# Order of the opening stages, bank-wise evacuation and earlier weight splits in a one-core HGRN2 layer

## Chip, cores and metric
One NeuronCore of a Trainium2 chip runs the whole layer. The metric is the device time of one execution, in microseconds, as the median of the runs.

## What is computed
One layer of a bidirectional generator trunk, all in float32, for 256 latent tokens `x` and 256 context tokens `ctx` of width 2048:
```
shift, scale, gate, shift2, scale2, gate2 = split(silu(c) @ w_ada + b_ada, 6)   # context: silu(c_ctx)
a     = rms_norm(t, norm_mix) * (1 + scale) + shift          # for x and ctx
q,v,g = split(a @ w_in, 3);   z[d] = a @ w_f[d]              # d = forward, backward
log_f = log_sigmoid(clip(z)) + log1p(lb * exp(-z));  k = (1 - lb) * sigmoid(-z);  q = silu(q) / sqrt(128)
o     = scan of S_t = diag(f_t) S_{t-1} + k_t v_t^T, o_t = S_t^T q_t, both directions, 16 heads of 128
h     = x + gate * ((rms_norm(o, o_norm) * silu(g)) @ w_o)
h     = h + gate2 * swiglu(rms_norm(h, norm_ffn) * (1 + scale2) + shift2);  out = rms_norm(h, final_norm)
```
The context is scanned first and gives the latent scan its start states. The inner width of the SwiGLU is 5632.

## The kernel before
**Products in three parts.** Each weight block is read as float32 into one of four slots of `raw` (128 x 1024, 512 KB) and split into `whi` (ACT, `hi`, L426) and `wlo = raw - whi` (DVE, `lo`, L689), three slots each. Activations stand as `ahi` and `alo` (features x 512 tokens, 16 column groups k of 128). A product is hi*hi + hi*lo + lo*hi, three matmuls (`three`, L1121).

**Head.** The first four of the six parts of `w_ada` (64 blocks, `rb` 0 to 63) are streamed; 40 are split, and 24 (`ada_direct`, k mod 8 in 1, 4, 6) go whole from slots of their own to a plain float32 matmul (L1066). `mod_sum` (L1054) sums rows of the modulation for c and c_ctx. A quarter q is 16 blocks; the column is (q + 2) mod 4, so scale comes before shift. After a quarter, ACT copies the rows (`mod_rows`, L440), PE turns them (`turn_rows`, L1080), DVE adds the bias (`modulation`, L716). At rb 6 (`X_AT`) ctx and x tiles are loaded, squared on ACT (`x_rstd`), transposed on PE (`turn_x`) and copied to `xT` by DVE (L737). At rb 16 SP stores the transposed x to DRAM (L365, 2 MB; it is read back for the residual), and DVE multiplies `xT` by the row norm in place (L746), after that store. At rb 32 `keep` and `masks` are loaded. Before all that, PE waits for the identity, the bias rows, o_norm and six vector rows, and transposes them (L1094, L1095); DVE copies them out (L696, L697), and ACT makes silu(c) (L432). `modulate(k)` (L463) applies scale and shift (L469) and makes `ahi` (L472), `a_lo(k)` (L728) makes `alo`: k 0 to 7 beside rb 56 to 63, k 8 to 15 after the last quarter.

**Pairs.** Sixteen heads make eight pairs (`positions`, L93). A pair has 8 chunks "VQ" (two k each; values into banks 0 and 1, queries into bank 2) and 8 chunks "Z" (gates of two directions and two heads, banks 0 to 3, matmuls of 512 columns). C_B is the first chunk. Between VQ and Z, DVE copies the values out of banks 0 and 1 (`values`, L814, L819) and ACT the queries by SiLU with a table load before and after (`queries`, L521). After Z, DVE clips the four gate banks (`clip_gates`, L788, L793), ACT makes exponentials (`gate_exps`, `gate_sigmoid`), DVE log gates and keys (L796 to L812). The scan of a head is 13 steps j, one per chunk position (`scan` on each of three engines), two heads overlapping. Of these: DVE cumulates the gates and sums the keys (j=0, L885 to L896), builds level exponents (j=1, 2), multiplies levels (j=3, 4, L855) and operands (j=5, L907); PE turns keys and makes scores (j=6, 8, L1227, L1230), states (j=7), outputs (j=9, L1238); DVE places masked scores (`place`, L860, at j=7 and 9, seven copies L867) and scales outputs (j=12, L935). PE's part stands in the middle of a chunk.

**Order at a position.** The engines walk the same list. DVE: `lo(ck)`, gates and keys, scan steps, `ada(i)` (an accumulation for the other modulation rows, L783), then at the boundaries `values` or `clip_gates`. ACT: `hi(ck)`, gate exps, scan steps, then `queries`. `hi(ck)` waits until chunk ck-3 has been used. SP issues the loads in the order of `RING`: chunk ck, then the `ada` blocks of ck; a load waits until the block four places before has been consumed.

**Rest.** A gate stage "G" (32 chunks, from C_G), the output projection (from C_WO, `wide`), SwiGLU (from C_FF), its down projection, and the final norm. The tail of the heads' scans runs in G.

The code of the Z and VQ matmuls and the loop that calls them:

Of the kernel before, what the change touches and what calls it, by code (L numbers as in the profile page):

```python
# [19 lines left out]
F32 = mybir.dt.float32  # L20
# [36 lines left out]
DIRECT = 6  # L57
X_AT = 6
# [9 lines left out]
R_NMIX, R_NFFN, R_FIN, R_LB, R_C, R_CCTX, R_ONORM = 0, 16, 32, 48, 64, 80, 96  # L68
VROWS = 97
# [35 lines left out]
def build(nc, x, c, ctx, c_ctx, w_ada, b_ada, norm_mix, norm_ffn, lb_logits, w_in, w_f, o_norm, w_o,  # L105
# [12 lines left out]
    with stack:  # L118
# [14 lines left out]
        xin = arena[:, 0:4 * D].rearrange("p (t d) -> p t d", t=4)  # L133
        h1 = arena[:, 0:KF * T].rearrange("p (k t) -> p k t", k=KF)
# [37 lines left out]
        vrow = arena[:, 4 * D:4 * D + P]  # L172
        brow = arena[:, 4 * D + P:4 * D + 2 * P]
# [27 lines left out]
        s_vrow = sem("vector_rows_in")  # L201
        s_keep = sem("keep_and_masks_in")
# [25 lines left out]
        s_used = sem("chunk_used")  # L228

# [66 lines left out]
        def _(sp):  # L296
            sp.dma_start(ident[:, :], ident_in).then_inc(s_const, 16)
            sp.dma_start(brow[0:96, :], b_ada[0].rearrange("(k p) -> k p", p=P)).then_inc(s_const, 16)
            sp.dma_start(vrow[R_ONORM:R_ONORM + 1, :], o_norm).then_inc(s_const, 16)
# [18 lines left out]
            def load(ck):  # L318
# [3 lines left out]
                if ck < C_B:  # L322

                    q, k = divmod(SPLIT_ADA[ck], KD)
                    col = (q + 2) % 4 * CW
# [26 lines left out]
            def load_direct(j):  # L352
                if j >= DIRECT:
                    sp.wait_ge(s_du, j - DIRECT + 1)
                q, k = divmod(DIRECT_ADA[j], KD)
                col = (q + 2) % 4 * CW
# [17 lines left out]
            for ck in range(C_B, CHUNKS):  # L374
                load(ck)
                for i in ada_blocks(ck):
# [43 lines left out]
        def _(act):  # L420
# [7 lines left out]
            for r, v in ((R_C, c[0]), (R_CCTX, c_ctx), (R_NMIX, norm_mix[0]), (R_NFFN, norm_ffn[0]), (R_FIN, final_norm),  # L428
                         (R_LB, lb_logits[0])):
                act.dma_start(vrow[r:r + KD, :], v.rearrange("(k p) -> k p", p=P)).then_inc(s_vrow, 16)  # L430
            act.wait_ge(s_vec, 1)
            act.activation(cs[:, :, 0], vec[:, R_C:R_C + KD], ACT.Silu)  # L432
            act.activation(cs[:, :, 1], vec[:, R_CCTX:R_CCTX + KD], ACT.Silu).then_inc(s_cs, 1)
            act.wait_ge(s_cs, 1)
            act.activation(cs4[:, :, :, 0], cs[:, :, :], ACT.Copy).then_inc(s_c4, 1)
            act.preload_act_table_set(EXP_LN)
            act.wait_ge(s_lb, 1)
            act.activation(lbt[:, 1, :], lbt[:, 0, :], ACT.Exp).then_inc(s_lb, 1)
# [24 lines left out]
            def modulate(k):  # L463

                act.wait_ge(s_mod, 8 if k < 8 else 10)
                act.wait_ge(s_xn, k + 1)
                for i in range(2):
                    v = xT[:, k, i * T:(i + 1) * T]
# [3 lines left out]
                act.activation(ahi[:, k, :], xT[:, k, :], ACT.Copy).then_inc(s_ah, 1)  # L472

            for rb in range(4 * KD):
                if rb == X_AT:
                    x_rstd()
                if not ada_direct(rb % KD):
                    hi(SPLIT_ADA.index(rb))
                if rb == 10:
# [4 lines left out]
                if rb >= 4 * KD - 8:  # L484
                    modulate(rb - 4 * KD + 8)
# [7 lines left out]
            for i in range(6, KD // 2 + 1):  # L493
# [21 lines left out]
            def gate_sigmoid(pr, i):  # L515
# [3 lines left out]
                act.activation(K, K, ACT.Exp, scale=-1.0).then_inc(s_zk, 1)  # L519

# [86 lines left out]
            for k in range(KD):  # L607
# [6 lines left out]
                hi(C_WO + 2 * k)  # L614
                if k == 0:
# [70 lines left out]
        def _(dve):  # L686
# [8 lines left out]
            dve.wait_ge(s_vecT, 1)  # L695
            dve.tensor_copy(vec[:, :], mx[:, 0:VROWS]).then_inc(s_vec, 1)  # L696
            dve.tensor_copy(bias[:, :], mx[:, 128:224]).then_inc(s_vec, 1)  # L697

# [704 lines left out]
```

## Time and profile before
| | |
|---|---|
| median of 3 runs | 1943.01 us (1941.77 to 1945.99) |
| the profiled execution's own time | 1942.41 us |
| its span | 1940.1 us, mean granted clock 0.990 |
| instructions | 31876 |
| first matmul into a bank of a pair | 124.30 us |
| DMA | 353.18 MB, mean 182 GB/s |

The profile is of one execution. "Busy" is the union of an engine's instructions. Matmuls are pipelined, so a duration overlaps the next one; pace is the distance of starts. PEclk is the granted share of 2.4 GHz: 1.0 or, throttled, 0.5 (1.2 GHz). In lists of waits the engine after "<-" released the one before it. In timelines the bracket holds the idle time of the engine before the instruction and what ended it.

### The profile page before, as it was taken

How to read it: one execution, taken by the hardware profiler on the slowest of the kernel's cores; microseconds unless marked ns; L12 is line 12 of the kernel's file. 1: busy time of each engine (PE TensorE's matmuls, PEld its weight loads, DVE VectorE, ACT ScalarE, POOL GpSimd, SP SyncE). 2: the span in 40 equal slices, each digit the busy share in tenths (PEclk: the TensorE clock that was granted, in tenths of full speed). 3: DMA queues.
4: the chain of work that ended last, by engine and by line, in shares of the span. 5: the costliest groups of instructions: out<-in, count | busy, mean ns of one | idle time of the engine just before them, and what ended most of it. 6: DMA issues, size and time to landing. Idle time of an engine off the chain costs nothing.

```text
span 1940.1 us, 31876 instructions
## 1 busy us (share of the span) xinstructions
PE 1852.1 (95%) x13318; PEld 1689.8 (87%) x13318; DVE 1256.8 (65%) x1949; ACT 861.9 (44%) x1186; POOL 0.2 (0%) x4
## 2 busy tenths in 40 slices
PE   6989999999999999999889999999999999999998
PEld 2258989788989788888779989999999999999996
DVE  4754768686968787878985455555545555545445
ACT  4582535343545344545445454333333433444444
POOL 0000000000000000000000000000000000000000
PEclk9999999999999999999999999999999999999999
DMA  8965544443444444443655546777767676555552
GB/s 326 392 217 167 170 128 138 141 153 125 147 131 131 157 147 130 142 141 120 196 185 209 183 123 206 216 227 217 217 218 218 214 225 212 182 182 183 182 185 98
DMA packets 175377, 353.18 MB, mean 182 GB/s; under 512 B 12737, under 2 KB 80642, under 8 KB 174594
## 3 DMA queue, kind: packets, MB, share of 16 engines
q1 hardware_dynamic: 175042, 351.11, 56.2%
q8 instruction: 104, 1.70, 0.4%
q14 instruction: 39, 0.32, 0.1%
q10 hardware_dynamic: 192, 0.05, 0.0%
HBM read 346.92 MB, written 4.19 MB: 181 GB/s over the span
## 4 chain that ended last, share of the span: by engine, by line
PE 79%; DVE 14%; DMA 2%; issue 2%; ACT 2%; ACTq 0%; DVEq 0%
PE bank L1122 19%; PE bank L1123 19%; PE bank L1124 19%; DVE wlo L689 3%; DVE aacc L783 3%; PE score L1227 2%; PE bank L1159 2%; PE bank L1161 2%; PE bank L1160 2%; DMA raw<-in_w_ada_dram 2%; PE score L1122 1%; PE score L1123 1%; PE score L1124 1%; DVE work L867 1%; DVE work L837 1%
## 5 line engine op out<-in xcount | busy, mean ns | idle before, releaser
L1122 PE MATMUL bank<-ahi,whi 128*128 128x256 f32 (+1 forms) x2912 | 891.8, 306 | 34.7 <-DVE wlo L689 19.0
L1123 PE MATMUL bank<-alo,whi 128*128 128x256 f32 (+1 forms) x2912 | 882.7, 303 | 0.0
L1124 PE MATMUL bank<-ahi,wlo 128*128 128x256 f32 (+1 forms) x2912 | 882.4, 303 | 0.0
L689 DVE TENSOR_TENSOR wlo<-raw,whi 128x1024 fp32r<-128x1024 f32 x496 | 605.7, 1223 | 417.6 <-ACT whi L426 417.0
L426 ACT ACTIVATE whi<-raw 128x1024 fp32r<-128x1024 f32 x496 | 522.3, 1056 | 547.8 <-PE bank L1124 447.1
L1122 PEld LDWEIGHTS bank<-ahi,whi 128*128 128x128 f32 x2912 | 560.3, 192 | 63.8 <-DVE wlo L689 22.7
L1124 PEld LDWEIGHTS bank<-ahi,wlo 128*128 128x128 f32 x2912 | 560.3, 192 | 20.7
L1123 PEld LDWEIGHTS bank<-alo,whi 128*128 128x128 f32 x2912 | 560.6, 193 | 18.5
L1159 PE MATMUL bank<-whi,ahi 128*128 128x256 f32 x512 | 151.1, 295 | 16.0 <-DVE arena L793 9.9
L783 DVE SCALAR_TENSOR_TENSOR aacc<-raw,cs,aacc 128x1024 f32<-128x1024 f32 x120 | 153.5, 1279 | 0.5
L1161 PE MATMUL bank<-whi,alo 128*128 128x256 f32 x512 | 146.2, 285 | 0.0
L1160 PE MATMUL bank<-wlo,ahi 128*128 128x256 f32 x512 | 146.2, 285 | 0.0
L1159 PEld LDWEIGHTS bank<-whi,ahi 128*128 128x128 f32 x512 | 99.7, 195 | 20.9 <-issue 12.6
L1160 PEld LDWEIGHTS bank<-wlo,ahi 128*128 128x128 f32 x512 | 99.7, 195 | 0.2
L1161 PEld LDWEIGHTS bank<-whi,alo 128*128 128x128 f32 x512 | 99.4, 194 | 0.0
L867 DVE COPY_PREDICATED work<-masks,score 128x128 f32<-128x128 uint32 x224 | 67.8, 303 | 7.7
L1122 PE MATMUL score<-ahi,whi 128*128 128x256 f32 x240 | 68.0, 283 | 0.5 <-DVE wlo L689 0.5
L1123 PE MATMUL score<-alo,whi 128*128 128x256 f32 x240 | 67.9, 283 | 0.0
L1124 PE MATMUL score<-ahi,wlo 128*128 128x256 f32 x240 | 67.9, 283 | 0.0
L570 ACT ACTIVATE rstd<-ob 128x256 f32<-128x256 f32 x16 | 6.1, 384 | 132.4 <-PE ob L1241 132.4
L1227 PE MATMUL score<-work 128*128 128x128 f32 x448 | 55.2, 275 | 0.0
L1227 PEld LDWEIGHTS score<-work 128*128 128x128 f32 x448 | 53.1, 192 | 0.5
(216 smaller groups left out, 1780.7 us busy)
## 6 DMA issues: line engine op xcount, KB each, us to landing
raw<-in_w_ada_dram SPq DMA_DIRECT2D x168, 512.0 KB, 3.9
raw<-in_ffn_w_gate_dram SPq DMA_DIRECT2D x88, 512.0 KB, 3.8
raw<-in_ffn_w_up_dram SPq DMA_DIRECT2D x88, 512.0 KB, 4.1
raw<-in_ffn_w_down_dram SPq DMA_DIRECT2D x88, 512.0 KB, 3.4
raw<-in_hg_w_in_dram SPq DMA_DIRECT2D x128, 256.0 KB, 3.1
raw<-in_hg_w_f_dram SPq DMA_DIRECT2D x128, 256.0 KB, 3.5
raw<-in_hg_w_in_dram SPq DMA_DIRECT2D x32, 512.0 KB, 4.6
raw<-in_hg_w_o_dram SPq DMA_DIRECT2D x32, 512.0 KB, 3.6
```

The costliest lines, as they stand in the source:

```text
L426: act.activation(whi[:, ck % SPL, :], raw[:, q % RAW, :], ACT.Copy).then_inc(s_hi, 1)
L689: dve.tensor_tensor(wlo[:, ck % SPL, :], raw[:, SEQ["w", ck] % RAW, :], whi[:, ck % SPL, :].bitcast(F32), ALU.subtract).then_inc(s_lo, 1)
L783: dve.scalar_tensor_tensor(out=aacc[:, :], in0=block, scalar=cs[:, k, 0:1], in1=aacc[:, :], op0=ALU.mult, op1=ALU.add).then_inc(s_ac, 1)
L837: last = dve.tensor_tensor(er, xr, r, ALU.subtract)
L867: dve.copy_predicated(pT[:, t, :], masks[:, li * P:(li + 1) * P], src).then_inc(s_pl, 1)
L1122: pe.matmul(dst, w, ah, start=start, stop=False, skip_group_check=True)
L1123: pe.matmul(dst, w, al, start=False, stop=False, skip_group_check=True)
L1124: return pe.matmul(dst, wl, ah, start=False, stop=stop, skip_group_check=True)
L1159: pe.matmul(dst, ahi[:, k, tk], whi[:, s, o], start=st, stop=False, skip_group_check=True)
L1160: pe.matmul(dst, ahi[:, k, tk], wlo[:, s, o], start=False, stop=False, skip_group_check=True)
L1161: last = pe.matmul(dst, alo[:, k, tk], whi[:, s, o], start=False, stop=end, skip_group_check=True)
L1227: last = pe.matmul(score[:, li // 4, (li % 4) * P:(li % 4 + 1) * P], ebuf[:, 0, li, t * P:(t + 1) * P], ebuf[:, 1, li, t * P:(t + 1) * P], ...
```

## The change
1. **c first.** c and c_ctx get a tile of their own, transposed to PSUM as soon as they and the identity are there; SiLU reads PSUM. The other vectors and the bias follow at rb 2 (SP's loads) and rb 6 (PE's transposes, DVE's copies); the lower-bound steps stand at rb 10 to 13, the exp table load at rb 5.
2. **Halves.** Quarters now go scale 1st half, shift 1st half, scale 2nd half, shift 2nd half (`ada_column`). `modulate` and `a_lo` for k 0 to 7 move to rb 40 to 55, each second block.
3. **x stored later.** The normed x goes to `xn` (over `xin` in the arena) and leaves `xT` whole; the store is issued behind the load of chunk C_B+6, `keep` and `masks` behind C_B+4. The first scan waits for both.
4. **Bank by bank.** At the first and last chunk of VQ and Z the units are ordered by bank; each finished bank gives a signal (`s_vd`, `s_zd`). `clip_gates` waits for each bank by itself and stands ahead of the position's scan steps; `values` moves from DVE to ACT.
5. **Split ahead.** At position ck, ACT and DVE split chunk ck+1 instead of ck, ahead of the scan steps. The `ada` blocks are loaded one chunk later in the ring.

```diff
+def ada_column(q):
+    return (2 * (1 - q % 2) + q // 2) * CW
...
+        xn = arena[:, 0:KD * TT].rearrange("p (k t) -> p k t", k=KD)
...
             for rb in range(4 * KD):
+                if rb == 2:
+                    sp.dma_start(brow[0:96, :], b_ada[0].rearrange("(k p) -> k p", p=P)).then_inc(s_vrow, 16)
+                    sp.dma_start(vrow[R_ONORM:R_ONORM + 1, :], o_norm).then_inc(s_vrow, 16)
...
-                if rb == KD:
-                    sp.wait_ge(s_xe, KD)
-                    sp.dma_start(xdram.rearrange("p (k t) -> p k t", k=KD), xT[:, :, T:TT]).then_inc(s_xs, 16)
-                if rb == 2 * KD:
-                    sp.dma_start(keep[:, :], keep_in).then_inc(s_keep, 16)
-                    sp.dma_start(masks[:, :], masks_in).then_inc(s_keep, 16)
...
             for ck in range(C_B, CHUNKS):
                 load(ck)
-                for i in ada_blocks(ck):
+                if ck == C_B + 4:
+                    sp.dma_start(keep[:, :], keep_in).then_inc(s_keep, 16)
+                    sp.dma_start(masks[:, :], masks_in).then_inc(s_keep, 16)
+                if ck == C_B + 6:
+                    sp.wait_ge(s_xe, KD)
+                    sp.dma_start(xdram.rearrange("p (k t) -> p k t", k=KD), xT[:, :, T:TT]).then_inc(s_xs, 16)
+                for i in ada_blocks(ck - 1) if ck <= C_WO else ada_blocks(ck):
                     load_ada(i)
...
@@ ACT
-                act.wait_ge(s_mod, 8 if k < 8 else 10)
+                act.wait_ge(s_mod, 6 if k < 8 else 11)
...
-                if rb >= 4 * KD - 8:
-                    modulate(rb - 4 * KD + 8)
+                if 40 <= rb < 56 and rb % 2 == 0:
+                    modulate(rb // 2 - 20)
...
+            def values(pr):
+                if pr >= 2:
+                    act.wait_ge(s_o, 2 * pr - 2)
+                for i in range(2):
+                    act.wait_ge(s_vd, 2 * pr + i + 1)
+                    act.activation(vals[pr % 2][:, 2 * i:2 * i + 2, :], bank[i][:, :].rearrange("p (t v) -> p t v", t=2),
+                                   ACT.Copy).then_inc(s_vev, 1)
...
                 if ck > C_B + KD // 2:
-                    hi(ck)
+                    hi(ck + 1)
+                if kind == "Z" and r == 0:
+                    values(u)
...
@@ DVE
                 if KD <= rb < 2 * KD:
                     k = rb - KD
                     if k == 0:
                         dve.wait_ge(s_rs, 7)
-                        dve.wait_ge(s_xs, 16)
-                    dve.tensor_tensor(xT[:, k, :], xT[:, k, :], rstd[:, :], ALU.mult).then_inc(s_xn, 1)
+                        dve.wait_ge(s_xt, KD)
+                    dve.tensor_tensor(xn[:, k, :], xT[:, k, :], rstd[:, :], ALU.mult).then_inc(s_xn, 1)
...
             def clip_gates(pr):
-                dve.wait_ge(s_used, C_B + 16 * (pr + 1))
...
                 for i, (d, h) in enumerate(UNITS):
+                    if i < 3:
+                        dve.wait_ge(s_zd, 3 * pr + i + 1)
+                    else:
+                        dve.wait_ge(s_used, C_B + 16 * (pr + 1))
...
                 if ck > C_B + KD // 2:
-                    lo(ck)
+                    lo(ck + 1)
+                p = (ck - C_B) % 16
+                if p == 0 and C_B + 16 <= ck <= C_G:
+                    clip_gates((ck - C_B) // 16 - 1)
...
-                if kind == "Z" and r == 0:
-                    values(u)
-                if p == 0 and C_B + 16 <= ck <= C_G:
-                    clip_gates((ck - C_B) // 16 - 1)
...
@@ PE
-            pe.wait_ge(s_const, 16 * 3)
-            pe.wait_ge(s_vrow, 16 * 6)
-            pe.transpose(mx[:, 0:VROWS], vrow[0:VROWS, :], ident[0:VROWS, 0:VROWS])
-            pe.transpose(mx[:, 128:224], brow[0:96, :], ident[0:96, 0:96]).then_inc(s_vecT, 1)
+            pe.wait_ge(s_const, 16)
+            pe.wait_ge(s_crow, 32)
+            pe.transpose(mx[:, 224:224 + 2 * KD], crow[:, :], ident[0:2 * KD, 0:2 * KD]).then_inc(s_cT, 1)
...
+            def chunk_vq(ck, r, u, between):
+                if r == 0:
+                    order = ((0, 0), (1, 0), (0, 2), (1, 2), (0, 1), (1, 1))
+                elif r == 7:
+                    order = ((0, 0), (1, 0), (0, 1), (1, 1), (0, 2), (1, 2))
+                else:
+                    order = ((0, 0), (0, 2), (0, 1), (1, 0), (1, 2), (1, 1))
...
+            def chunk_z(ck, r, u, between):
+                if r == 0:
+                    order = [(a, f) for f in (3, 0, 1, 2) for a in range(2)]
+                elif r == 7:
+                    order = [(a, f) for f in (0, 2, 1, 3) for a in range(2)]
+                else:
+                    order = [(a, f) for a in range(2) for f in (3, 0, 1, 2)]
...
-    RING += [("a", _i) for _i in ada_blocks(_ck)]
+    RING += [("a", _i) for _i in (ada_blocks(_ck - 1) if _ck <= C_WO else ada_blocks(_ck))]
```
In an order, (a, f) is the k within the chunk and the bank; the scan steps of PE stand in the middle.

## Rows read from the trace of the kernel before
**Rows 1.** The page's first part: busy time and share of each engine, instructions.
```profile
PE 1852.1 (95%) x13318; PEld 1689.8 (87%) x13318; DVE 1256.8 (65%) x1949; ACT 861.9 (44%) x1186; POOL 0.2 (0%) x4
```
**Rows 2.** Table by stage: stretch, length, busy by engine, PEclk, DMA share, GB/s.
```profile
0.00:124.30 124.30, 99.72 (x348) 26.83 (x349) 76.28 (x107) 72.20 (x95) 0.20 (x4) 0.98 0.90 345
...
900.00:1000.00 100.00, 78.11 (x604) 74.73 (x604) 93.62 (x178) 56.21 (x94) 0.00 (x0) 0.97 0.58 184
...
1200.00:1300.00 100.00, 100.00 (x836) 100.00 (x835) 54.88 (x48) 38.78 (x39) 0.00 (x0) 1.00 0.72 221
```
**Rows 3.** Waits of PE from 130 us on: total us, times, longest.
```profile
PE bank L1122 <- DVE wlo L689: 19.0, 12, 3.0
PE bank L1122 <- DVE arena L819: 11.0, 6, 2.8
PE bank L1159 <- DVE arena L793: 9.9, 7, 2.7
PE bank L1159 <- DVE wlo L689: 4.6, 7, 0.7
PE ob L1238 <- DVE work L867: 4.1, 8, 1.0
```
**Rows 4.** Timeline and one stage row around the transposes of x.
```profile
22.25 1.92 ACT L452 ACTIVATE alo<-arena 128x2048 fp32r<-128x2048 f32 x1 [0.17 <-DMA arena<-in_x_dram]
...
23.64 9.66 DVE L737 COPY work<-bank 128x512 f32<-128x512 f32 x16 [5.98 <-PE bank L1105]
...
34.46 0.33 SPq L303 DMA_DIRECT2D raw<-in_w_ada_dram  x1
...
23.00:34.50 11.50, 10.38 (x70) 7.01 (x69) 10.86 (x18) 5.99 (x11) 0.00 (x0) 1.00 0.66 262
```
**Rows 5.** Table by stage: the weight stream, and the start of the first pair.
```profile
90.00:100.00 10.00, 10.00 (x32) 2.08 (x31) 5.55 (x5) 6.11 (x7) 0.00 (x0) 1.00 1.02 402
...
130.00:140.00 10.00, 10.00 (x86) 10.00 (x85) 5.83 (x7) 9.84 (x18) 0.00 (x0) 1.00 0.17 54
```
**Rows 6.** Timeline of ACT from 104 us, and PE's first matmul of a pair.
```profile
104.02 1.06 ACT L426 ACTIVATE whi<-raw 128x1024 fp32r<-128x1024 f32 x1 [0.23 <-DMA raw<-in_w_ada_dram]
...
106.63 0.59 ACT L469 ACTIVATE work<-work,modc,scl 128x256 f32<-128x256 f32 x1
...
124.30 0.58 PE L1159 MATMUL bank<-whi,ahi 128*128 128x256 f32 x1 [1.51 <-DVE wlo L689]
```
**Rows 7.** Timeline of PE in the third pair: its idle time.
```profile
330.20 0.49 PE L1238 MATMUL ob<-work,arena 128*128 128x128 f32 x2 [0.54 <-DVE work L867]
334.66 0.39 PE L1159 MATMUL bank<-whi,ahi 128*128 128x256 f32 x1 [0.72 <-DVE wlo L689]
343.48 0.50 PE L1122 MATMUL bank<-ahi,whi 128*128 128x512 f32 x1 [2.84 <-DVE arena L819]
```
**Rows 8.** ACT's reading of the query bank there, and the stretches before and behind.
```profile
341.59 0.60 ACT L528 ACTIVATE arena<-bank 128x512 f32<-128x512 f32 x1
...
324.40:344.00 19.60, 14.78 (x109) 13.39 (x109) 19.30 (x39) 9.18 (x10) 0.00 (x0) 1.00 0.54 163
344.00:394.70 50.70, 50.59 (x252) 42.02 (x251) 35.89 (x71) 15.83 (x28) 0.00 (x0) 1.00 0.45 140
```
**Rows 9.** The two VQ phases behind long clip gaps: gap, and stages.
```profile
397.44 0.55 PE L1159 MATMUL bank<-whi,ahi 128*128 128x256 f32 x1 [2.66 <-DVE arena L793]
...
396.60:429.75 33.15, 32.31 (x250) 32.34 (x251) 28.46 (x53) 19.19 (x36) 0.00 (x0) 0.90 0.48 150
703.00:734.66 31.66, 31.07 (x250) 31.10 (x251) 28.22 (x52) 19.07 (x36) 0.00 (x0) 0.95 0.49 155
```
**Rows 10.** Table by stage: two other stretches with the low clock.
```profile
646.50:652.50 6.00, 5.64 (x13) 4.46 (x14) 5.44 (x13) 5.01 (x14) 0.00 (x0) 0.50 0.59 189
1000.00:1004.50 4.50, 4.50 (x27) 4.50 (x26) 4.50 (x10) 1.48 (x2) 0.00 (x0) 0.62 0.67 179
```
**Rows 11.** Timeline of PE: the last wait of the gate stage.
```profile
999.58 0.38 PE L1122 MATMUL bank<-ahi,whi 128*128 128x256 f32 x1 [3.03 <-DVE wlo L689]
```

More of the change, by code:

```diff
@@ L492, in _ @@
                     hi(C_B + k // 2 - 2)
-            for i in range(6, KD // 2 + 1):
+            for i in range(6, KD // 2 + 2):
                 hi(C_B + i)
@@ L1124, in three, with v_bank @@
                 return pe.matmul(dst, wl, ah, start=False, stop=stop, skip_group_check=True)
+            def v_bank(ck, r, a, u, half):
+                s, k = ck % SPL, 2 * r + a
+                first, end = k == 0, k == KD - 1
+                if first and u:
+                    pe.wait_ge(s_zc, 4 * (u - 1) + 1 + 2 * half)
+                o = slice(512 * a, 512 * a + 256)
+                for t in (2 * half, 2 * half + 1):
+                    dst = bank[half][:, (t % 2) * T:(t % 2 + 1) * T]
+                    tk = slice(t * P, (t + 1) * P)
+                    st = first and t % 2 == 0
+                    pe.matmul(dst, ahi[:, k, tk], whi[:, s, o], start=st, stop=False, skip_group_check=True)
+                    pe.matmul(dst, ahi[:, k, tk], wlo[:, s, o], start=False, stop=False, skip_group_check=True)
+                    last = pe.matmul(dst, alo[:, k, tk], whi[:, s, o], start=False, stop=end, skip_group_check=True)
+                return last
@@ new lines, in q_bank @@
+            def q_bank(ck, r, a, u):
+                s, k = ck % SPL, 2 * r + a
+                first, end = k == 0, k == KD - 1
+                if first and u:
+                    pe.wait_ge(s_zc, 4 * (u - 1) + 2)
+                for f in range(2):
+                    o = slice(512 * a + 256 + f * P, 512 * a + 256 + (f + 1) * P)
+                    last = three(bank[2][:, f * T:(f + 1) * T], whi[:, s, o], wlo[:, s, o],
+                                 ahi[:, k, T:TT], alo[:, k, T:TT], first and f == 0, end)
+                return last
@@ new lines, in beside @@
+            def beside(ck, between):
+                for j, n in between:
+                    scan(j, n)
+                for e in ada_ends(ck):
+                    sum_modulation(e)
+                if ck == C_B:
+                    turn_rows(pe, 3)
+            def chunk_vq(ck, r, u, between):
[5 more added lines that the diff above has]
+                    order = ((0, 0), (0, 2), (0, 1), (1, 0), (1, 2), (1, 1))
+                for i, (a, f) in enumerate(order):
+                    if i == 3:
+                        beside(ck, between)
+                    k = 2 * r + a
+                    if u == 0:
+                        pe.wait_ge(s_al, k + 1)
+                    last = q_bank(ck, r, a, u) if f == 2 else v_bank(ck, r, a, u, f)
+                    if r == 7 and a == 1 and f < 2:
+                        last.then_inc(s_vd, 1)
+                last.then_inc(s_used, 1)
@@ L1130, in chunk @@
                     if a:
-                        for j, n in between:
-                            scan(j, n)
-                        for e in ada_ends(ck):
-                            sum_modulation(e)
-                        if ck == C_B:
-                            turn_rows(pe, 3)
+                        beside(ck, between)
                     k = 2 * r + a
                     first, end = k == 0, k == KD - 1
-                    if ck < C_B + 8 and kind == "VQ":
-                        pe.wait_ge(s_al, k + 1)
@@ new lines, in chunk @@
+                    tk = slice(T, TT) if kind == "G" else slice(0, T)
+                    bb = 2 * (u % 2)
+                    for f in range(4):
+                        if kind == "G" and u == 0 and first and f % 2 == 0:
+                            pe.wait_ge(s_zc, 4 * (PAIRS - 1) + 1 + f)
+                        o = slice(512 * a + f * P, 512 * a + (f + 1) * P)
+                        last = three(bank[bb + f // 2][:, (f % 2) * T:(f % 2 + 1) * T], whi[:, s, o], wlo[:, s, o],
+                                     ahi[:, k, tk], alo[:, k, tk], first and f % 2 == 0, end)
```

201 lines of the change are left out of this document (96 added, 105 removed).

## The prediction
> **What bounds the kernel now.** The engine totals come first: PE is busy 95% of the span, DVE 65%, ACT 44% [rows 1]. The change takes no matmul away, so it can win only time in which PE stands still or runs at the low clock. The table by stage says where [rows 2]: before 124.3 us PE does only preparation, beside a DMA at 0.90; the gate stage (900 to 1000) has 78% PE beside 94% DVE; from 1200 on PE is full and nothing can be won. The list of waits names the rest [rows 3]: behind the first bank matmul PE waits for splits of weights (19.0 and 4.6 us), value copies (11.0), clips (9.9) and masked placing (4.1), some 49 us. The low clock (1.2 GHz, 0.5 granted) adds to that, behind long gaps [rows 9, 10].
>
> **The head.** It is a stream of weights: at 402 GB/s [rows 5] a block of 512 KB takes 1.30 us.
> - *Start and c first.* PE gets to the transposes of x only at 23, when the last x tile has landed too (22.25), so all 16 DVE copies (9.66 us) follow; the splits wait behind them, the next load is issued at 34.46, and the DMA has run dry (262 GB/s in 23 to 34.5) [rows 4]. With only c's two rows and the identity awaited, PE starts 4 to 5 us earlier, is at the transposes by 18 or so and keeps up with the tiles. That leaves the last four copies (2.4) and the two copies of vectors (0.5; L696 and L697, moved there) behind 22.25, and the load at 28.4: **6.0 us** (bounds 0 and 6.4).
> - *Store, keep, masks* leave the stream: 2.10 + 0.72 MB by 402 GB/s = **7.0**. They come back behind chunks C_B+4 and C_B+6, on SP's queue ahead of the loads of C_B+5 and C_B+7; the DMA does 54 GB/s there [rows 5], and the first scan, which waits for both, is 20 chunks off. Zero; without that cover 7.0 again.
> - *Halves of scale and shift.* Now no column of `a` can be modulated before three quarters are summed. From 105 on eight modulates stand between ACT's last splits: from the start of the split at 104.02 to that of the second modulate is 2.61, 0.96 for the split and 1.65 for a modulate. The first bank matmul starts at 124.30 [rows 6]. After the change they run at blocks 40 to 55. Behind the split at 104.02 the stream then has seven blocks and C_B's, 8 x 1.30 = 10.4, then 2.3 for C_B's split by ACT and DVE: 116.7 against 124.30, **7.6**. In exchange ACT has in those 16 blocks 10 splits and 8 modulates, 9.6 + 13.2 = 22.8, and a pair of row copies (1), against 20.8 of DMA: 0 to 4 lost, part hidden by loads in flight. I take **-2.0**.
>
> Head: 6.0 + 7.0 + 7.6 - 2.0 = **18.6**.
>
> **Inside the pairs.**
> - *VQ to Z.* At 343.48 PE waits 2.84 for a value copy [rows 7], which stands in DVE's queue behind a split, level products and an accumulation: DVE is busy 19.3 of the 19.6 us from 324.4 to 344 [rows 8]. Now ACT copies each bank as it is summed, two of some 0.60, as its own read of a bank takes [rows 8]; bank 3 goes first in Z and covers them. Behind them on ACT stands the query SiLU with its table load; it ended at 342.2 [rows 8], and bank 2 is wanted last, six of eight units (4.1 us) into a Z that now starts at about 340: 1.9 to spare, 0.7 if both copies pushed it. All 11.0 goes. So do the waits for a split behind the placing step (0.72 at 334.66 [rows 7], four such), 2.9. Three before it don't: placing follows PE's scores by the same chain, sum of keys, accumulation, split, mask copies, whatever chunk is split, so the wait at 330.20 (0.54 [rows 7]) grows by what is saved before it. **13.9**.
> - *Z to VQ.* Seven waits for clips, 9.9 [rows 3]. Three banks are clipped while PE still sums the fourth, so PE does not stop. But clips now precede DVE's level products and accumulation (3.2), of which three clips (1.8) are made up: DVE starts its next position 1.4 later against the end of Z. The five short gaps (4.5 in all) then lose 1.2: **3.3**. The two long ones (2.66 at 397.44 and its like at 703.6) stand with a low clock, 0.90 in the mean of 33 us and 0.95 of 32, 3.4 and 1.7 lost [rows 9]. There DVE binds instead: it is busy 28.5 of 33.15 and 28.2 of 31.66 us up to its sum of keys [rows 9], 4.7 and 3.4 idle. Less 0.5 each for slivers, PE can win 4.2 of 6.1 and 2.9 of 4.4. **7.1**.
> - *Clock.* The low clock at 646.5 [rows 10] stands behind a value-copy gap, in a Z phase, where DVE has room (35.9 of 50.7 busy in the like [rows 8]): 6.8 at half, **3.4**.
>
> **The gate stage.** DVE's work sets its length. The clip gap ahead of it, 0.9. With each split one position ahead, PE leaves DVE's last heavy position a chunk earlier: the gap of 3.03 at 999.58 ends with a split that stood behind level products [rows 11], and a chunk is 24 matmuls at 100/836 us [rows 2] = 2.9. Of DVE's 6.4 us of idleness [rows 2] I take 3.3 back, since PE is further on, and the low clock after 1001 (0.62 [rows 10]) gives 1.7. **8.8** (bounds 3.8 and 11).
>
> The new order of units in Z and VQ has the same matmuls: nothing. From C_WO on only one split is ahead, and PE is full: nothing.
>
> **Sum**: 18.6 + 13.9 + 3.3 + 7.1 + 3.4 + 8.8 = 55.1, off the profiled execution's own 1942.4 (span 1940.1): **1887.3**. The median, 1943.0, is 0.6 above that execution; the range holds that.
>
> **A rule against the recovered clock.** The gap of 2.84 at 343.48 has no low clock before or behind it (1.00 in both stretches [rows 8]); The Trainium skill says otherwise (TensorE: Matmul & The Clock Gate, "A second HAM failure mode: psum-queue depth-cycling"): frequent short idle spells between groups of matmuls are enough to make the clock oscillate. By it the placing waits that stay (up to 1.2, once a phase) would keep the falls; the trace so far does not agree.
>
> **Rivals.**
> - *DVE becomes the bound of the pairs* (0.17). If what I call slack is a chain with PE's scores, gaps only move into the placing wait (L1238). For: DVE at 94% in the gate stage and without a pause before 344. Against: 14.8 us idle in the Z phase that follows [rows 8]. Head 18.6 and half of the other 36.5: 1942.4 - 36.9 = 1906.
> - *The head gives half* (0.13): PE's start does not matter, or ACT at blocks 40 to 55 starves the loads. 1887.3 + 9 = 1896.
> - *The falls of the clock stay* (0.08). Then the two long clip gaps give 5.3 of the 7.1, and the 3.4 and the 1.7 are not won: 6.9 less, 1894. It is the rule's case.
> - *Slower* (0.03): the tether. ACT's split of chunk ck+1 needs PE to have ended ck-2, and DVE now stands at that split (2.3 with ACT's) ahead of the scan steps of ck; ACT's exps stand behind it too, where before they had a chunk more of lead. If PE then waits at its scan steps, the loss repeats at 144 positions (pairs 1 to 7 and the gate stage) and decides from 55.1/144 = 0.38 us each; at 0.45 it is 65: 1952. Against: PE's waits for scan work are 4.1 in all [rows 3].
> - *Better than forecast* (0.05): ACT's crowding is hidden (2.0), DVE binds neither kind of clip gap (3.4 + 1.2), the gate stage gives its 11 (2.2): 1878.
>
> **How the numbers follow.** Forecast 0.54, rivals as given. The likeliest case alone spans 1880 to 1896 (head -4/+2, gate stage -5/+2, pairs +3). With the cases at 1896, 1894, 1906 and 1878 the range is 1875 to 1908. 0.2%, about 4 us, can just be told from no change here. Faster by more 0.96, within 0.01, slower 0.03.
>
> **What would show it.** Head: no dip of GB/s between 23 and 35, next load near 28, first bank matmul at 104 to 108; at 112 or later, if ACT shows no waits for DMA at blocks 40 to 55. Pairs: no wait of PE for value copies or clips; the placing wait larger, 5 to 9 us in all; waits for splits near none before 900; no low clock between 390 and 720. Gate stage: some 90 us. I am wrong if PE waits at L1238 or L1227 for tens of us, if it waits for ACT's value copies, or if DVE's idle time in VQ phases turns to waits for ACT's split.

## The result, and the profile after

The changed kernel takes 1894.13 us (1888.60 to 1899.08 in four runs) against 1943.88 for the kernel before on the same chip: a ratio of 0.9739, interval 0.9722 to 0.9756. The profiled execution took 1894.17, its span is 1892.2. Forecast were 1887.3 and a range of 1875 to 1908: the sign and the range held, the saving was 48 us (profiled execution against profiled execution) where 55 were summed up.

The page's first part, which answers to [rows 1], and the table by stage (stretch, length, busy by engine, PEclk, DMA share, GB/s), which answers to [rows 2]:

```profile
PE 1839.9 (97%) x13319; PEld 1689.6 (89%) x13319; DVE 1248.2 (66%) x1935; ACT 877.4 (46%) x1202; POOL 0.2 (0%) x4
```
```profile
0.00:111.12 111.12, 97.16 (x349) 26.69 (x350) 76.81 (x109) 71.05 (x92) 0.20 (x4) 1.00 0.97 359
...
856.37:900.00 43.63, 36.56 (x286) 35.90 (x285) 42.19 (x86) 25.82 (x45) 0.00 (x0) 0.92 0.48 148
900.00:950.00 50.00, 43.13 (x335) 42.46 (x334) 48.84 (x93) 27.96 (x45) 0.00 (x0) 0.93 0.70 228
950.00:1003.14 53.14, 49.57 (x400) 48.82 (x398) 29.59 (x48) 25.17 (x35) 0.00 (x0) 0.97 0.57 191
```

The head now has the DMA at 0.97 (0.90 before). In the gate stage DVE is even fuller than before, 97 and 98% of the first 94 us, and the granted clock is at 0.92 to 0.97.

The waits of PE over the whole span (total us, times, longest), which answer to [rows 3]; the second line lies in the head, where [rows 3] does not reach:

```profile
PE ob L1313 <- DVE work L892: 17.6, 8, 5.1
PE score L1099 <- DVE wlo L717: 6.3, 4, 2.9
PE bank L1150 <- DVE wlo L717: 4.8, 3, 2.1
```

Value copies, clips, and splits inside the pairs have gone from the list. From the first bank matmul to the gate stage PE's waits were 28.7 us in 27; they are 8.4 in 6, all at the placing step (L1313). The other 9.2 of the 17.6 are two waits in the gate stage.

Where the time went, by four starts in PE's timeline:

| start of | before | after | gained on the way |
|---|---|---|---|
| first bank matmul | 124.30 | 111.12 | 13.2 (forecast 18.6) |
| first matmul of the gate stage | 901.10 | 856.37 | 31.5 (28.6: 13.9 + 3.3 + 7.1 + 3.4, and the clip gap of 0.9) |
| first matmul of the output stage | 1051.36 | 1003.14 | 3.5 (7.9) |
| end | 1940.1 | 1892.2 | -0.3 (0) |

### The profile page after: what moved, and what is told of

Same layout as the page of the kernel before. It is cut to its first block, busy times and chain, and to the rows that moved or that the text cites. A ratio compares the mean times of both kernels' runs of the same rounds, so it can differ in the third digit from the quotient of the medians.

```text
span 1892.2 us, 31881 instructions
## 1 busy us (share of the span) xinstructions
PE 1839.9 (97%) x13319; PEld 1689.6 (89%) x13319; DVE 1248.2 (66%) x1935; ACT 877.4 (46%) x1202; POOL 0.2 (0%) x4
## 4 chain that ended last, share of the span: by engine, by line
PE 81%; DVE 12%; issue 3%; ACT 2%; DMA 2%; SPq 0%; DVEq 0%; ACTq 0%
PE bank L1150 19%; PE bank L1151 19%; PE bank L1152 19%; DVE wlo L717 3%; PE bank L1165 2%; PE bank L1166 2%; PE bank L1167 2%; PE score L1302 2%; DVE work L892 2%; DVE aacc L813 2%; PE score L1150 2%; PE score L1152 2%; PE score L1151 2%; DMA arena<-in_x_dram 1%; PE ob L1152 1%
## 5 line engine op out<-in xcount | busy, mean ns | idle before, releaser
L682 ACT ACTIVATE ahi<-arena 128x256 fp32r<-128x256 f32 x44 | 18.4, 417 | 76.1 <-PE ob L1152 76.1
L1302 PEld LDWEIGHTS score<-work 128*128 128x128 f32 x448 | 53.1, 192 | 0.5
```

Source lines behind the costliest of these rows:

```text
L682: act.activation(yhi[:, k % 2, :], h1[:, k, :], ACT.Copy).then_inc(s_yh, 1)
L1302: last = pe.matmul(score[:, li // 4, (li % 4) * P:(li % 4 + 1) * P], ebuf[:, 0, li, t * P:(t + 1) * P], ebuf[:, 1, li, t * P:(t + 1) * P], ...
```

## The experiments

Each starts from the changed kernel. "Head" below is the start of the first bank matmul, "middle" is from there to the first matmul of the output stage (892.0 us in the changed kernel, 927.1 in the one before). Both come from the one profiled execution of each, and the middles of the changed kernel and of the five that differ from it in the head alone lie between 888.6 and 892.0, so that differences of up to 3.4 us in it are no finding. The experiments ran on several chips, so each ratio is taken against the kernel before on the same chip; differences in us are from the changed kernel's 1894.13.

### The head

**Store, keep and masks back in the stream.**

```
 for rb in range(4 * KD):
+    if rb == KD:
+        sp.wait_ge(s_xe, KD); sp.dma_start(xdram..., xT[:, :, T:TT])
+    if rb == 2 * KD:
+        sp.dma_start(keep...); sp.dma_start(masks...)
```


> The changed kernel, with the store of x back ahead of block 16 and keep and masks back ahead of block 32, as before the change. Theory A (the head is bound by bytes, as the forecast had it): 2.82 MB more at 402 GB/s, the first bank matmul 7.0 us later than the 111.12 of the changed kernel, so at 118. Theory B (since the change DVE binds from about 50 to 60 and ACT from 74 to 97, because the multiplies and the modulates stand thick there, and the stream only follows them): the store falls ahead of those stretches, where the loads in flight are ahead by up to four blocks, keep and masks in the stretch behind the first; part of the 7.0 is hidden, first bank matmul at 113 to 116. Total time by A 1901, by B 1896 to 1899.

1901.84 us (1900.03 to 1903.87), ratio to before 0.9782 [0.9759, 0.9805]; head at 117.81, 6.7 later. The 2.82 MB cost nearly what they take on the DMA, 7.0 by the forecast, although ACT is as full behind them as in the changed kernel (11.87 of 12 us from 85 to 97 in both). Theory A holds for this term. The granted clock is at 0.83 from 35 to 50 and 0.91 from 50 to 60 in this run alone, beside a stream of 405 and 308 GB/s (382 and 317 in the changed kernel); whether it has a part in the 6.7 was not taken apart.

**Modulates late.**

```
-    if 40 <= rb < 56 and rb % 2 == 0: modulate(rb // 2 - 20)
+    if rb >= 4 * KD - 8: modulate(rb - 4 * KD + 8)
```
DVE's `a_lo` moves with them.

> The changed kernel with the eight first modulates back at blocks 56 to 63 instead of every second block from 40 to 54 (scale and shift still by halves). The forecast had 7.6 gained by the move and 2.0 lost to crowding of ACT, so undoing it alone costs 5.6: first bank matmul at 116.7. Theory B (crowding took more than 2.0: about 7, so that the move gained nearly nothing): first bank matmul within 2 us of 111.1, with ACT's splits no longer behind their data between 74 and 97, landings dense there, and the delay at blocks 56 to 63 in its place.

1896.21 us (1894.60 to 1901.31), ratio 0.9754 [0.9732, 0.9777]; head at 113.29, 2.2 later and not 5.6. The table by stage says why. In the changed kernel:

```profile
74.00:97.00 23.00, 20.13 (x69) 4.53 (x68) 15.24 (x20) 22.75 (x37) 0.00 (x0) 1.00 0.97 357
```
and with the modulates late:

```profile
85.00:97.00 12.00, 12.00 (x45) 3.08 (x44) 7.39 (x13) 8.99 (x13) 0.00 (x0) 1.00 1.03 410
97.00:112.00 15.00, 10.60 (x32) 2.00 (x30) 9.11 (x11) 14.81 (x25) 0.00 (x0) 1.00 0.61 213
```

In the middle of the head ACT is busy 22.75 of 23 us and the stream runs at 357 GB/s; without modulates there it runs at 388 (74 to 85) and 410 (85 to 97), and what it wins is lost again behind 97, where ACT is the bound. Moving them was worth 2.2, not 5.6.

**Multiplies spread.** `if KD <= rb < 2 * KD` becomes `if 11 <= rb < 43 and rb % 2 == 1`, `k = rb // 2 - 5`.

> The changed kernel with the sixteen multiplies of x by its norm at every second block from 11 to 41, instead of at each block from 16 to 31. DVE then has no stretch in which it is the bound. If DVE's crowding from 50 to 60 cost stream time that is not made up (theory B): first bank matmul 2 to 3 us earlier, at 108 to 109, total 1891 to 1892. If the stream is bound by bytes, or what DVE lost is hidden by ACT's crowding behind it (both are waited for by the same loads): no change at 111.1.

1893.70 us (1891.88 to 1894.51), ratio 0.9736 [0.9717, 0.9754]; head at 109.07, 2.1 earlier. From 50 to 60 us DVE was busy all the time and the DMA down at 317 GB/s; spread, it is 8.13 busy of 10 and 372 GB/s. So DVE's own crowding held the stream, a cost that my sum did not have. In total time the gain is within the scatter of the runs.

**Modulates spread**, at every third block from 38: `if 38 <= rb < 62 and rb % 3 == 2: modulate(rb // 3 - 12)`, with DVE's `a_lo` one block behind each.

> The changed kernel with its first eight modulates at every third block from 38 to 59 instead of every second from 40 to 54. ACT then has 16 splits, 8 modulates and a pair of row copies in 24 blocks: 16 x 0.96 + 8 x 1.65 + 1 = 29.6 us against 24 x 1.28 = 30.7 us of stream, and no longer bounds it. Theory B (ACT's crowding cost some 4 us from 74 to 97): first bank matmul 3 to 4 us earlier, at 107 to 108, total 1890. Theory A (the stream is not held by ACT): no change.

1893.68 us (1891.50 to 1895.88), ratio 0.9737 [0.9717, 0.9757]; head at 112.04, 0.9 later. A miss: I had looked at ACT's sum of work and not at what the first modulate waits for. ACT's timeline:

```profile
72.85 0.60 ACT L481 ACTIVATE arena<-arena,modc,scl 128x256 f32<-128x256 f32 x1 [3.43 <-DVE modc L741]
```

At block 38 its scale and shift are not summed yet. ACT stands 3.43 us with landed blocks behind it, and between 74 and 85 the DMA falls to 293 GB/s.

**c with all rows**: `pe.wait_ge(s_vrow, 16 * 6)` ahead of c's transpose, with the rows of biases issued first.

> The changed kernel with c's transpose waiting for all rows of vectors again, the rows of the biases issued first, as before the change (silu and the rest of its order kept). The forecast put the start at 6.0 us with the x copies; the next load was issued 5.1 us earlier than before (29.36 against 34.46). Theory (start and stream move together): PE's first weights matmul from 7.9 back to 11 to 13, the load behind the x copies 3 to 5 us later, first bank matmul at 114 to 116, in all 1897 to 1899. Rival: the loads in flight and DVE's crowded stretch from 50 to 60 behind it absorb the later start: first bank matmul at 111 to 112.5, total within 2 us of 1894.

1892.23 us (1890.57 to 1899.07), ratio 0.9739 [0.9706, 0.9772]; the head at 114.22, 3.1 later. The load behind the x copies, in SP's timeline of the changed kernel and of this one:

```profile
29.36 0.33 SPq L314 DMA_DIRECT2D raw<-in_w_ada_dram  x1
```
```profile
32.17 0.33 SPq L316 DMA_DIRECT2D raw<-in_w_ada_dram  x1
```

2.8 us of the 5.1 that this load came earlier (34.46 [rows 4]) are thus c's own rows; the rest came with the other orders of the start. The total does not show the 3.1: the middle of this execution is 3.4 shorter, 1.6 of it in the pairs, where the clock is at 0.94 against 0.91 from 660 to 715 (more on this below), and 1.8 in the gate stage. The head terms are therefore read from the start of the first bank matmul, not from totals.

### Pairs and gate stage

**Split not ahead**: `hi(ck + 1)` and `lo(ck + 1)` become `hi(ck)` and `lo(ck)`, the ring as before.

> The changed kernel with each chunk split at its own position again (the accumulation's blocks back at the place in the ring that they had). The forecast gave splitting ahead 2.9 us behind the placing steps and 2.9 of the gate stage: by it this run is 5.8 us slower than the changed kernel (1900), with PE's waits for wlo back at 0.7 each behind the placing steps, and near 3 at the end of the gate stage. Rival: the split stands in the placing chain either way, so that the placing wait (17.6 us in 8 in the changed kernel) falls by what the waits for splits grow, and the time stays within 2 us. A third way: more than 10 us slower, if the clips and value copies pay only with splits ahead.

1927.51 us (1925.21 to 1927.66), ratio 0.9910 [0.9895, 0.9925]: 33.4 us slower, the third way. The middle is 925.3, against 927.1 of the kernel before. PE's waits from the first bank matmul to the gate stage:

```profile
PE bank L1163 <- DVE wlo L716: 13.7, 17, 1.2
PE bank L1148 <- DVE wlo L716: 11.8, 7, 1.9
PE ob L1311 <- DVE work L891: 2.3, 6, 0.5
```

27.8 us, nearly as much as the 28.7 of the kernel before. There are no waits for value copies or clips, where the kernel before had 21.8 us of them; the waits for splits are 25.5 where it had 4.6, so nearly all has come back as a wait for a split. ACT's timeline at such a place, and PE's:

```profile
323.65 0.60 ACT L543 ACTIVATE arena<-bank 128x512 f32<-128x512 f32 x1 [1.21 <-PE bank L1165]
...
324.97 1.91 ACT L583 ACTIVATE work<-work 128x2048 f32<-128x2048 f32 x1
326.89 1.28 ACT L553 ACT_TABLE_LOAD   x1
328.19 0.60 ACT L553 ACTIVATE arena<-bank 128x512 f32<-128x512 f32 x1
328.80 1.28 ACT L555 ACT_TABLE_LOAD   x1
330.09 1.06 ACT L440 ACTIVATE whi<-raw 128x1024 fp32r<-128x1024 f32 x1
```
```profile
332.46 0.50 PE L1148 MATMUL bank<-ahi,whi 128*128 128x512 f32 x1 [1.62 <-DVE wlo L716]
```

ACT now waits for PE's sums of values, then does exps and the queries with two table loads, and the split for the next chunk stands behind all of it. A queue that is made to wait for the end of PE's chunk needs the next chunk's split ahead of that wait.

**Values on DVE**: the two copies go back behind DVE's scan steps, waiting for the whole chunk.

> The changed kernel with the value copies back on DVE behind its scan steps of that position, both waiting for the whole chunk. The forecast gave their move 11.0 us. Two units of bank 3 now run first in Z instead of one (0.7 us more of cover, in six pairs 4 us), so by the forecast 7 to 11 us slower: 1901 to 1905, with PE's waits for vals in six Z phases of 1 to 2.5 us each. Rival: DVE has since come further ahead of PE there, because it need not wait for PE before the split, and the copies are hidden: within 2 us of 1894.

1912.69 us (1910.73 to 1914.17), ratio 0.9839 [0.9822, 0.9857], 18.6 slower. PE waits for them 14.6 us in 7, longest 3.4, where the kernel before waited 11.0 in 6 [rows 3]. The run takes back the engine and the signal for each bank together; which of the two does it was not run. So moving the copies was worth more than their old waits: PE no longer loses 4.6 us for splits on the way to Z, and would meet DVE's queue the earlier (this reason is argued, no run takes it apart).

**Clips late**: back at the end of DVE's position, waiting for the whole chunk.

> The changed kernel with the clips back at the end of DVE's position and waiting for the whole last chunk of Z. The forecast gave the early clips 3.3 (five short gaps) + 7.1 (two long ones with their clocks) + 0.9 (before the gate stage) = 11.3 us: 1905 by it. Rival: part of what was gained at the two long gaps came from the splits ahead and not from the clips, since DVE's own queue ends earlier there by a split: 5 to 7 us slower, 1900. If a long gap comes back, a low clock may stand behind it (3.4 us each).

1900.40 us (1896.73 to 1903.60), ratio 0.9773 [0.9754, 0.9792], 6.3 slower, as the rival had it. The clip waits are back with 10.8 us in 7, longest 3.1, and the placing waits in the pairs fall from 8.4 to 4.2. That is what a chain on PE's scores does: what PE does not wait for at the clips it waits for, in part, at the placing.

**Split ahead alone**: both of the last two edits together.

> The changed kernel with both the value copies and the clips back at the end of DVE's position, each waiting for the whole chunk, so that of the three edits of the pairs only the split ahead is left. Undone alone, the value copies cost 18.6 us and the clips 6.3, the split ahead 33.4, in all 58 where the pairs and the gate stage gained 35. If values and clips add up (theory: what is not additive lies between each of them and the split ahead), this is 1894 + 25 = 1919, and the split ahead is worth about 11 without the other two against 33 with them. Rival: it is less than additive, since both gaps are work that DVE does late in the same queue: 1912 to 1915.

1919.24 us (1918.23 to 1920.22), ratio 0.9865 [0.9841, 0.9888]; 25.1 slower, the sum of the two (24.9). Middle: 919.6. With the kernel before at 927.1 the four corners of the square are

| middle, us | split at its own position | split ahead |
|---|---|---|
| values and clips late | 927.1 (before) | 919.6 |
| values and clips early | 925.3 | 892.0 |

Alone they gain 1.8 and 7.5; together 35.1. The 1.8 lies inside the scatter of 3.4, so all that can be said of it is that it is small. The corner of the kernel before is not quite the changed kernel with all three undone: the three other corners also have the new order of units in VQ and Z, and the store of x, `keep` and `masks` behind the first chunks. No run takes the order of units back by itself; what it is worth is open.

**Placing first.** Not an undo: DVE's placing step j = 9 runs ahead of the rest of its position, and the accumulation of the position before behind it.

```
+    for j, n in tasks:
+        if j == 9: scan(j, n)
+    for i in late: ada(i)
     lo(ck + 1)
```


> Not an undo: the changed kernel with DVE's second placing step (j = 9) ahead of everything else in its position, and the accumulation of the position before deferred behind it. In the changed kernel the chain from PE's score to the placed block is 5.7 us: sum of keys 0.3 behind its wait, accumulation 1.2, split 1.14, keys 0.4, diagonal and seven mask copies 2.8. Theory (this chain is what PE waits for at L1313, 8.4 us in six pairs, 9.2 in two of the gate stage): the chain becomes 3.0, shorter than the PE work of 4.2 or more that covers it; the six waits vanish, and the low clock behind the one at 696.6 too: 8.4 to 13 us less before 856. In the gate stage DVE is the bound, the waits move to other steps: 0 to 3. In all 1881 to 1886. Rival: the split of the next chunk, now behind the placing, is late instead, and PE waits for it at the next chunk: 1891 to 1895.

1882.04 us (1881.53 to 1882.79), ratio 0.9680 [0.9665, 0.9694]: 12.1 less than the changed kernel. DVE's timeline in the changed kernel:

```profile
307.12 0.43 DVE L922 TENSOR_TENSOR work<-arena 128x256 f32<-128x256 f32 x1 [1.81 <-PE score L1305]
307.46 1.28 DVE L813 SCALAR_TENSOR_TENSOR aacc<-raw,cs,aacc 128x1024 f32<-128x1024 f32 x1
308.66 1.22 DVE L717 TENSOR_TENSOR wlo<-raw,whi 128x1024 fp32r<-128x1024 f32 x1
309.79 0.48 DVE L845 TENSOR_SCALAR arena<-arena,oml 128x512 f32<-128x512 f32 x1
310.19 0.28 DVE L888 TENSOR_TENSOR work<-score,ident 128x128 f32<-128x128 f32 x1
310.50 2.30 DVE L892 COPY_PREDICATED work<-masks,score 128x128 f32<-128x128 uint32 x7
```
and here:

```profile
307.37 0.43 DVE L922 TENSOR_TENSOR work<-arena 128x256 f32<-128x256 f32 x1 [1.80 <-PE score L1316]
307.71 0.28 DVE L888 TENSOR_TENSOR work<-score,ident 128x128 f32<-128x128 f32 x1
308.03 2.33 DVE L892 COPY_PREDICATED work<-masks,score 128x128 f32<-128x128 uint32 x7
```

5.7 us from PE's score to the placed block are now 3.0. The placing waits in the pairs fall from 8.4 to 1.7, and the granted clock is 1.00 over the pairs. From the first bank matmul to the gate stage it is 733.0 us against 745.25: of the 12.2, PE's idle time gives 6.0 (8.4 to 2.4) and the fall of the clock behind 696.56, which is gone, 4.7 (below). In the gate stage the waits only changed places (from the placing to the split, 11.7 in 8), as expected; 146.5 us against 146.8.

**Head and placing**: placing first, multiplies spread, and modulates at every third block from 40.

> Three orders together on the changed kernel: placing first (12.1 us of the span alone), multiplies at every second block from 11 (2.1), modulates at every third block, but from 40 on, so that the first finds its scale and shift ready (from 38, ACT stood 3.4 us for them and the gain was spent). Theory: the head gains 2.1 for DVE and 3 to 4 for ACT, first bank matmul at 105.5 to 107; total 1882 - 5 = 1877. Rival: the head's stream is by then bound by its bytes, ACT's share gives under 1: first bank matmul at 108 to 109, total 1880.

1877.81 us (1877.10 to 1880.38), ratio 0.9654 [0.9631, 0.9678]; head at 108.31, as the rival had it, while the total is the theory's 1877 (the gain on placing first alone is 3.1 at the first bank matmul, 3.4 in the spans and 4.2 in the medians). From 74 to 97 ACT is busy 20.16 of 23 and the stream at 385 GB/s, 28 more than in the changed kernel, but most of that came to no earlier start: 0.8 beyond what the multiplies gave.

**Sums before the gate**: in addition `ADA_ENDS` ends with 118, 134 in place of 131, 150, and the last two rows' sixteen blocks lie densest in the Z phases of pairs 6 and 7.

> The kernel of the run before in this list, and the accumulations of the last two modulation rows moved out of the gate stage: twelve of sixteen each in the Z phases of pairs 6 and 7, where DVE idles 10 to 14 us of 51. It takes about 15 accumulations of 1.17 us, 17.5 us, from DVE in the gate stage, where it is busy 94 to 97% of the first 94 us. Theory (DVE's work sets the length there): 12 to 16 us less between 856 and 1003, PE's waits in that stage go from some 15 us to under 5; total 1862 to 1866. Rival: there it is a chain of PE, ACT and DVE steps with waits among them, not DVE's sum of work, and Z phases of pairs 6 and 7 grow: 2 to 5 us less.

1873.74 us (1873.56 to 1876.27), ratio 0.9631 [0.9604, 0.9657]; on the same chip the run before it had 1877.10 to 1880.38. The gate stage, first without and then with the sums moved away:

```profile
841.25:987.60 146.35, 127.30 (x1018) 124.02 (x1016) 120.69 (x226) 79.18 (x123) 0.00 (x0) 0.98 0.59 192
```
```profile
845.95:984.20 138.25, 125.15 (x1000) 122.67 (x1001) 104.41 (x211) 78.08 (x122) 0.00 (x0) 0.96 0.46 148
```

DVE lost 16.3 us of work and the stage 8.1, and 5.2 were given back between the first bank matmul and the stage: each of the two Z phases is 1.7 longer, mostly by two new waits for clips (1.5 each), and the VQ phase between them 1.9, with one of the column sums of the moved rows on PE (16 matmuls, 1.7 us). The total, 4.1 less, is the rival's. For the cause neither theory holds alone: DVE's sum was the bound, since taking work from it shortened the stage; that behind half of the way it is ACT's chain is read from one wait, and no run moves ACT's work. The granted clock of the stage is also lower, 0.96 against 0.98. The longest wait left behind the head, on PE, and what DVE waited for:

```profile
935.22 0.58 PE L1161 MATMUL bank<-ahi,whi 128*128 128x256 f32 x1 [4.50 <-DVE wlo L717]
```
```profile
933.94 1.22 DVE L717 TENSOR_TENSOR wlo<-raw,whi 128x1024 fp32r<-128x1024 f32 x1 [4.19 <-ACT whi L440]
```

ACT does the gate's SiLUs there between two table loads of 1.28 and then two small steps and eleven small exps, all ahead of its split. This is the fastest version that ran, 1.1% below the changed kernel.

## Why the prediction was right in sign and range, and where it was not

**Start and c first (6.0).** The load came at 29.36, not 28.4, 5.1 us earlier than before. The terms that I named give 26.3 and not 28.4: 22.25 + 2.4 + 0.5, and 1.2 from the last copy to the load as before [rows 4]; 2.1 had no source. What bound it in the end was not a copy: the last tile of x landed at 23.25, and DVE, with its copies done, waited for ACT, which still had the row norms ahead of its split:

```profile
28.11 2.36 DVE L717 TENSOR_TENSOR wlo<-raw,whi 128x1024 fp32r<-128x1024 f32 x2 [0.77 <-ACT whi L440]
```

c's rows alone are worth 3.1 at the first bank matmul. What the other orders of the start give there was not run by itself; if the undone parts add up, 13.2 - 6.7 - 2.2 = 4.3 is left for the whole step, and 1.2 for them.

**Store, keep, masks (7.0).** 6.7. Right, the zero for where they went to included: no wait stands behind C_B+4 to C_B+7.

**Halves and modulates (7.6 less 2.0).** 2.2, where 5.6 were forecast. This is the step of the head that failed: the stream was taken to pass ACT's crowded blocks for 2.0. I set 22.8 us of ACT's work against 20.8 of DMA and let loads in flight hide some. The sum of ACT's work in the head is the same wherever the modulates stand: ahead of 97 they slow the stream, behind it they delay the last splits. And I did not cost DVE's multiplies at blocks 16 to 31, which hold the stream from 50 to 60: 2.1. "112 or later, if ACT shows no waits for DMA at blocks 40 to 55" was the sign I named; the start was 111.12, and between 74 and 97 ACT shows none.

**Value copies, splits behind placing (13.9), clips (3.3 + 7.1).** The waits went as said. The placing waits are 17.6 us in all, not 5 to 9; inside the pairs 8.4. The step said that the wait at 330.20 grows by what is saved before it, and that is what it did, but I allowed it 1.2 at most and it reached 2.31 in two phases. Against this, 21 waits fewer gave more than their idle time: from one matmul's start to the next a wait costs 0.16 more than the gap shown (at the wait of 0.47, 503.59 to 504.34 is 0.75 where the pace is 0.12, so it costs 0.63), some 3.4 us which I had not counted. With the 20.3 us of waits and 3.4 of clock (next paragraph) that is 27 of the 31.5; the rest was not taken apart. As terms of a sum the parts are not what I made of them, though. I gave the split ahead 2.9 in the pairs and 2.9 in the gate stage; the square above gives it 7.5 alone and 33.3 beside the others.

**Clock (3.4, and in 7.1 and 8.8).** The falls of the kernel before did go, and others came. In the pairs, behind a placing wait that is new:

```profile
696.56 0.49 PE L1313 MATMUL ob<-work,arena 128*128 128x128 f32 x2 [2.31 <-DVE work L892]
```
```profile
408.60:420.60 12.00, 11.90 (x92) 11.55 (x93) 11.14 (x26) 6.51 (x8) 0.00 (x0) 1.00 0.41 130
696.50:708.50 12.00, 11.94 (x62) 11.94 (x63) 7.63 (x19) 2.96 (x4) 0.00 (x0) 0.57 0.25 80
```

0.57 over 12 us is a fall to 1.2 GHz for 10.2 us, 5.1 lost by the clock's share. From the wait to the same later matmul (L1320) it is 12.25 us here and 7.55 at the place without a fall, so 4.7 in time. Before, 17 us of the pairs were at half (8.5 lost by the share), of which I had counted on 5.2: the 3.4, and 1.8 inside the 7.1. In the gate stage it falls at the waits of 5.05 (890.11), 4.17 (933.13) and 2.07 us (952.97). By the PEclk of its three stretches above, 0.08 x 43.6 + 0.07 x 50 + 0.03 x 53.1 = 8.6 us are lost by the share, against 0.03 x 100 + 0.38 x 4.5 = 4.7 before [rows 2, 10]. That is no measure of what it cost there. The stage up to the last long wait for a split, of the kernel before, the changed kernel and placing first:

```profile
901.10:999.58 98.48, 77.46 (x601) 74.28 (x601) 92.33 (x176) 55.11 (x93) 0.00 (x0) 0.97 0.57 181
856.37:952.97 96.60, 80.59 (x625) 79.06 (x623) 93.08 (x180) 56.39 (x94) 0.00 (x0) 0.93 0.59 188
844.37:940.72 96.35, 78.64 (x626) 75.89 (x624) 93.28 (x181) 56.60 (x94) 0.00 (x0) 0.98 0.60 190
```

DVE is busy 93.1 of the 96.6 us, so at most 3.5 can be the clock's or any wait's, and placing first, at 0.98 and with another order on DVE, is only 0.25 shorter. How much of the 3.5 is the clock's was not taken apart; the five kernels that differ in the head alone have the whole stage at 144.8 to 146.1 us against 146.8.

**The gate stage (8.8).** It gave 3.5 where 7.9 stood (8.8 less the clip gap of 0.9). Up to that wait, 98.48 became 96.60: of the 3.3 that I took from DVE's idleness 1.9 came. Behind it, 51.78 (999.58 to 1051.36) became 50.17 (952.97 to 1003.14), and it is 50.17 in placing first too:

```profile
999.58:1051.36 51.78, 51.27 (x417) 50.93 (x417) 28.53 (x47) 23.30 (x30) 0.00 (x0) 0.97 0.58 199
952.97:1003.14 50.17, 48.67 (x392) 48.13 (x392) 27.54 (x46) 22.56 (x29) 0.00 (x0) 0.97 0.58 196
```

The chunk of lead is there, one chunk of 24 matmuls fewer behind the wait (2.9), but the low clock behind it stayed (0.97 in both, where I had 1.7 gained), and a wait of 1.0 is new, for ACT's step behind the gate's SiLU and its two table loads:

```profile
983.24 0.70 PE L1320 MATMUL mx<-rstd,ones 128*128 128x256 f32 x2 [0.99 <-ACT rstd L595]
```

So of the 4.4 missing, 1.4 are idleness of DVE that was not won (the low clock ahead of the wait may have a part in it), 1.7 the clock behind the last wait for a split, and 1.0 the new wait for ACT.

So the rival in which the falls stay, given 0.08, is nearest to what happened to the clock, though the falls at the clip gaps that it kept are gone and others came; that the time is its 1894 is chance. The Trainium skill (TensorE: Matmul & The Clock Gate, "A second HAM failure mode: psum-queue depth-cycling") lays such oscillation on short idle spells between groups of matmuls. In the runs with placing first the pairs have 1.7 us of such waits and no fall, and there the trace agrees; the wait of 2.31 at 408.70 with no fall behind it does not fit it.

**The rivals.** "The head gives half" came closest to the head (13.2 of 18.6). "DVE binds the pairs" did not come: the pairs gave more than forecast. The tether cost nothing that the waits show. 1894 was the sum of misses of both signs: head -5.4, pairs +2.9, gate stage -4.4, rest -0.3.

## What to carry to other kernels

Ask of each engine's queue not only how long a moved step is, but what it now waits for and which producer stands behind it: early evacuations were worth 1.8 us (no more than the scatter) without the splits ahead of them and 27.6 with them. Undoing parts one at a time gives values that do not add up (33 + 19 + 6 for a gain of 35); two parts and their four corners do. And when a wait vanishes, put the step that is waited for next first in its queue: here that was worth 12 us for a dozen lines, nearly 5 of them by a fall of the clock that no longer came. In a stage where another engine is busy nearly all the time, PE's low clock costs at most that engine's idle time, not its own share.

## What the runs showed of the hardware

The same wait at the same place does not always bring the low clock. Behind the placing wait of 2.31 us at 408.70 the changed kernel kept 1.00, behind its like at 696.56 it fell. In the kernel with late modulates, which differs only in the head, it was the other way round; the wait and the stretches behind it and behind the second:

```profile
410.67 0.49 PE L1314 MATMUL ob<-work,arena 128*128 128x128 f32 x2 [2.31 <-DVE work L893]
```
```profile
410.50:422.50 12.00, 11.83 (x61) 11.83 (x62) 7.88 (x19) 2.88 (x4) 0.00 (x0) 0.57 0.27 85
```
```profile
703.20:715.20 12.00, 11.94 (x92) 11.59 (x93) 11.11 (x26) 6.54 (x8) 0.00 (x0) 1.00 0.41 130
```

With c's rows waited for, the second had 0.72 over 12 us. So in the pairs a fall is worth 0 to 5 us by a shift of 2 to 3 us in time, and a change of 3 us upstream can vanish from the total, as c's did. In the first 96 us of the gate stage, where DVE is busy 97%, a granted clock of 0.93 and one of 0.98 went with nearly the same time (96.60 and 96.35).

The runs of the changed kernel scatter over 10.5 us, those with placing first, which have the fewest such waits, over 1.3. Every execution has its mean granted clock on record, and in the changed kernel it goes with the span: 0.994 at 1886.8 us, 0.992 at 1892.2 and 1892.3, 0.989 at 1897.3. The difference of 0.005 of some 1890 us is 9.5 us lost by the clock's share, of a difference of 10.5 in span. So most of the scatter is the clock; which falls made it is not shown, since only one execution of each kernel was profiled in full.
